# Group B of the trunk step: score tiles in the idle value ring, projection four slots sooner, second norm's statistics by column tile, new slot numbers

## The reference, cut to what matters

```python
sh1, sc1, gt1, sh2, sc2, gt2 = adaln(c, w_ada, b_ada)
h = rmsnorm(x, g_norm1) * (1.0 + sc1) + sh1
q, k, v, u, g = jnp.split(h @ w_in, IN_SPLITS, axis=-1)      # 2048 -> 5120 columns
u = gelu(u); vn = layernorm(gelu(g), ln_v_g, ln_v_b)
att, gate_v, states = mixer(q, k, v, vn)   # 8 heads of 128, dilated windows, ALiBi; samples read 2048 cached rows
x = x + gt1 * (concat([att, u * gate_v]) @ w_out)
h2 = rmsnorm(x, g_norm2) * (1.0 + sc2) + sh2
x = x + gt2 * peer_ffn(h2, w_query, sub_keys, expert_u, expert_v)
return rmsnorm(x, g_final), states
```

## Time and profile before

| | us |
| --- | --- |
| median of 3 runs | 3785.51 (3781.29 to 3787.98) |
| profiled execution, its own time | 3779.13 |
| its span, first to last instruction | 3777.4 |
| busy: PE / DVE / POOL / ACT | 3104.6 / 2353.0 / 980.1 / 572.1 |
| bytes moved by DMA | 1344.8 MB, mean 356 GB/s |
| mean granted TensorE clock | 0.903 |

### The profile page before, as it was taken

The page is one execution under the profiler, slowest core; times in us unless marked ns, Lnnn a source line. Parts: engine busy times, 40 slices in busy tenths (PEclk is TensorE's granted clock), DMA queues, the critical chain, the costliest instruction groups (busy, mean ns, idle before and its releaser), DMA issues.

```text
span 3777.4 us, 28728 instructions
## 1 busy us (share of the span) xinstructions
PE 3104.6 (82%) x9975; PEld 1850.8 (49%) x9975; DVE 2353.0 (62%) x3580; ACT 572.1 (15%) x1365; POOL 980.1 (26%) x779
## 2 busy tenths in 40 slices
PE   4899997979996668796885885359996589999996
PEld 1333443733343434333674553347773257777774
DVE  3110114889986854548777777877777838656653
ACT  0000111121111445402242000420000000000000
POOL 3000001234333421233313323333223314222220
PEclk8999998979998679897996997579998899999998
DMA  9999655889989799988989999889999989999993
GB/s 310 398 361 367 233 200 202 338 319 403 409 330 361 262 401 415 397 296 336 367 292 358 416 416 386 283 341 417 417 417 416 416 333 417 416 417 417 417 411 132
DMA packets 326129, 1344.80 MB, mean 356 GB/s; under 512 B 27625, under 2 KB 76777, under 8 KB 217593
## 3 DMA queue, kind: packets, MB, share of 16 engines
q0 software_dynamic: 106912, 749.72, 49.8%
q1 hardware_dynamic: 166090, 549.84, 37.9%
q10 hardware_dynamic: 52984, 43.42, 3.5%
HBM read 1303.07 MB, written 38.96 MB: 355 GB/s over the span
## 4 chain that ended last, share of the span: by engine, by line
PE 57%; DMA 20%; DVE 15%; issue 4%; ACT 3%; POOL 0%; SPq 0%; ACTq 0%; DVEq 0%; POOLq 0%
PE ps L1023 27%; PE ps L619 7%; DVE arena L2183 7%; DMA arena<-in_expert_u_dram,arena 6%; DMA arena<-in_expert_v_dram 5%; PE ps L778 4%; PE ps L828 4%; DMA arena<-in_cache_k_dram 3%; PE ps L710 3%; PE ps L577 2%; DMA arena<-in_w_ada_dram 2%; DMA arena<-in_w_in_dram 2%; PE ps L607 2%; PE ps L1015 2%; DMA arena<-in_w_out_dram 1%
## 5 line engine op out<-in xcount | busy, mean ns | idle before, releaser
L1023 PE MATMUL ps<-arena 128*128 128x512 f32 x3072 | 1384.4, 611 | 175.2 <-DMA arena<-in_expert_v_dram 116.1
L2183 DVE CUSTOM_DVE_ANT_0 arena<-arena 128x2048 f32<-128x2048 f32 x544 | 1241.7, 2290 | 315.3 <-DMA arena<-in_expert_u_dram,arena 309.5
L1023 PEld LDWEIGHTS ps<-arena 128*128 128x128 f32 x3072 | 943.6, 309 | 615.0 <-issue 270.9
L2448 POOL DMA_INDIRECT arena<-in_expert_u_dram,arena x544 | 760.6, 1398 | 1760.9 <-DVE arena L2183 1567.0
L2096 DVE SCALAR_TENSOR_TENSOR arena<-arena 128x2048 f32<-128x2048 f32 x158 | 371.6, 2352 | 205.3 <-issue 165.8
L828 PE MATMUL ps<-arena 128*128 128x512 f32 x896 | 409.4, 611 | 0.4 <-DVE arena L2027 0.2
L619 PE MATMUL ps<-arena 128*128 128x512 f32 x640 | 288.4, 604 | 9.5 <-DMA arena<-in_w_in_dram 9.5
L828 PEld LDWEIGHTS ps<-arena 128*128 128x128 f32 x896 | 169.7, 195 | 246.6 <-issue 240.1
L2448 POOL DMA_INDIRECT arena<-in_expert_v_dram,arena x160 | 176.7, 1105 | 410.5 <-DVE arena L2096 368.3
L577 PE MATMUL ps<-arena 128*128 128x128 f32 (+3 forms) x954 | 158.4, 319 | 151.7 <-DMA arena<-in_cache_k_dram 50.3
L577 PEld LDWEIGHTS ps<-arena 128*128 128x128 f32 (+3 forms) x954 | 128.0, 169 | 220.2 <-issue 67.7
(11 more groups left out here) (246 smaller groups left out, 1761.1 us busy)
## 6 DMA issues: line engine op xcount, KB each, us to landing
arena<-in_expert_v_dram SPq DMA_DIRECT2D x320, 512.0 KB
arena<-in_w_ada_dram SPq DMA_DIRECT2D x96, 1024.0 KB, 10.5
arena<-in_w_in_dram SPq DMA_DIRECT2D x80, 1024.0 KB, 8.2
arena<-in_w_query_dram SPq DMA_DIRECT2D x36, 1024.0 KB
arena<-dense_coefs SPq DMA_DIRECT2D x48, 768.0 KB
arena<-in_w_out_dram SPq DMA_DIRECT2D x32, 1024.0 KB, 5.1
dense_coefs<-arena ACTq DMA_DIRECT2D x12, 2048.0 KB, 20.4
arena<-in_cache_k_dram SPq DMA_DIRECT2D x24, 1024.0 KB
```

The lines of the kernel that those rows point to most:

```text
L1023: ins = MM(ps[:, BANK[half, b] + c, :], weights, dense_v[m % V_DENSE][:, c * NC:(c + 1) * NC], start=(m == FIRST_TILE[half, b]), stop=(m = ...
L2183: V.tensor_tensor_reduce(out=u_slot[s % RING], in0=u_slot[s % RING], in1=h2[b], scale=1.0, scalar=0.0, op0=ALU.mult, op1=ALU.add, accum_ou ...
L2448: nc.gpsimd.indirect_dma_start(out=slot, out_offset=None, in_=table, in_offset=bass.IndirectOffsetOnAxis(ap=idx, axis=0),).then_inc(loaded ...
```

## The change

- Block 0's scores of heads 2 to 7 go to R0 + 6 D and block 1's scores to R0 + 7 D, which are buffers of the `expert_v` ring that is idle until slot 408; heads 0 and 1 of block 0 go to `sc_first` at HB0. ACT's wait ahead of the "hb" turns drops from six heads' choices to two. Two other waits go (ACT in `mix_b`, SP ahead of a load of near values); one comes (ACT, before quad 8 of block 0 is copied into `stage`, for all choices of block 1, as the staging buffer lies over the scores).
- T_TURN1 and T_IN are 4 slots lower; all that hangs on T_IN moves with it.
- The choices of block 0 are due at 0, 4, 15, 21, 29, 37, 46, 55 in place of 0, 4, 17, 19.6, 23.2, 26, 36, 42; those of block 1 every 8 slots from 62 in place of every 7 from 52.
- A batch of `sample_keys` has 2.6 slots in place of 3.6, its key steps 0.3 apart in place of 0.4 (far ones from 1.4 in place of 2.0). The due times of `sample_values`, counted from the batch's end, stay as they were.
- `project_out` has 2.4 slots a quarter in place of 1.8; T_OUT goes from 202.75 to 191.75, T_NORM2 from 231.95 to 229.75, T_QB from 240.45 to 235.75.
- Second norm: `bn_stats` is taken of each column tile as it is added (into `delta`, which is free by then), and only the three `mean_square_end` stand at T_NORM2. The stores of x to `x_mid` are issued by ACT, three per column tile, in place of SP, three in all. The modulate calls are due 1, 2 and 3 slots after T_NORM2 in place of 4, 5 and 6.

```diff
-T_TURN1 = 30.0
-T_IN = 33.8
+T_TURN1 = 26.0
+T_IN = 29.8
 def t_key(n):
     h = n % H
-    return T_S + 2.0 + 3.6 * (n // H) + (0.4 * h if h < 4 else 2.0 + 0.4 * (h - 4))
+    return T_S + 2.0 + 2.6 * (n // H) + (0.3 * h if h < 4 else 1.4 + 0.3 * (h - 4))
-T_OUT = t_soft(DECB - 1) + 5.0
+T_OUT = t_soft(DECB - 1) + 6.0
 def t_out(n, q):
-    return T_OUT + 1.8 * (4 * n + q)
-T_NORM2 = t_out(OUT_T - 1, 3) + 2.2
-T_QB = T_NORM2 + 8.5
+    return T_OUT + 2.4 * (4 * n + q)
+T_NORM2 = t_out(OUT_T - 1, 3) + 2.0
+T_QB = T_NORM2 + 6.0
-TOP_0 = [0, 4.0, 17.0, 19.6, 23.2, 26.0, 36.0, 42.0]
+TOP_0 = [0, 4.0, 15.0, 21.0, 29.0, 37.0, 46.0, 55.0]
     if b == 1:
-        return 52 + 7.0 * h + piece
+        return 62 + 8.0 * h + piece
-        sc_sb = [at(off, PH, 2, NKEY) for off in (HB0, F0, MIX0, MIX0 + D, F0)]
-        sc_last = at(MIX0 + D + NC, 2, 2 * NKEY)
+        sc_sb = [at(off, PH, 2, NKEY) for off in (R0 + 6 * D, R0 + 7 * D, MIX0, MIX0 + D, F0)]
+        sc_first = at(HB0, 2, 2, NKEY)
@@ turns_b on ACT
-                        act.wait_ge(idx_ready, heads_of(0, PH - 2))
+                        act.wait_ge(idx_ready, heads_of(0, 2))
@@ mix_b on ACT
-                act.wait_ge(idx_ready, heads_of(0, PH))
@@ project_out on ACT
+                    yield t_out(n, 3) + 1.9
+                    act.wait_ge(outb_free, 2 * (n + 1))
+                    wait_turn_taken(act, ("of", n))
+                    cols = slice(n * NC, (n + 1) * NC)
+                    for i, b in enumerate((2, 3, SB)):
+                        act.dma_start(x1_of[b][:, cols], x_b[i][0:ROWS[b], cols]).then_inc(x1b_stored, 16)
@@ build_dense on ACT
+                        if n == 8:
+                            act.wait_ge(idx_ready, heads_of(1, PH))
@@ project_out on DVE
                         if b == SB:
                             turn_taken(ins, ("of", n))
+                            wait_turn_taken(dv, ("of", n))
                         else:
                             ins.then_inc(outb_free, 1)
+                            dv.wait_ge(outb_free, 2 * n + i + 1)
+                        link(V.bn_stats(out=st_b[i][0:r, 6 * n:6 * n + 6], in_=x_b[i][0:r, cols]))
+                yield T_NORM2
                 for i in range(3):
-                    yield T_NORM2 + i
-                    if i == 0:
...
-                    mean_square(7 + i, x_b[i])
+                    mean_square_end(7 + i, st_b[i])
                 for i in range(3):
-                    yield T_NORM2 + 4.0 + i
+                    yield T_NORM2 + 1.0 + i
                     if i == 0:
                         dv.wait_ge(mod2b_loaded, 64)
-                        dv.wait_ge(x1b_stored, 48)
+                        dv.wait_ge(x1b_stored, 48 * OUT_T)
@@ SP
                 else:
                     sp.wait_ge(u_done, SLOTS)
-                    sp.wait_ge(idx_ready, heads_of(1, PH))
...
-            sp.wait_ge(x1b_done, 1)
-            for i, b in enumerate((2, 3, SB)):
-                sp.dma_start(x1_of[b], x_b[i][0:ROWS[b], :]).then_inc(x1b_stored, 16)
```

More of the change, by code:

```diff
@@ L464, in trunk_step @@
         gate2_kept, gfin_kept, gate2_kept_s = at(MIX0, D), at(MIX0 + D, D), at(F0, D, rows=NS)
+        st_b = [delta[:, 24 * i:24 * i + 24] for i in range(3)]
         def heads_of(b, h):
@@ L1799, in _ @@
                 x1_tile(n, 0)
-            mean_square_end(2, 16)
+            mean_square_end(2)
             dv.sem_inc(x1a_done, 1)
```

34 lines of the change are left out of this document (15 added, 19 removed).

## The result

The changed kernel takes **3821.45 us** (median of 4 executions, 3814.17 to 3822.14) where the kernel before takes 3783.40 on the same chip (3776.54 to 3787.98): a ratio of 1.0098, 95% interval 1.0077 to 1.0118. It is 29 to 45 us slower. The profiled execution spans 3812.4 us, the one before 3777.4, both at a granted clock of 0.90.

A forecast was written before the change was run, and what follows sets the result against it. No engine was taken to bound the whole; what counts is when the stream reaches about slot 386. 23 - 11 - 4 + 12 - 14 + 8 = 14 us faster, 3771 us on the median's scale, range 3733 to 3797.

The forecast's parts named there:

- attention's first score product: Start to attention: PE reaches attention 23 us sooner (14 if nothing is gained, 32 if PE loses no weights wait).
- 14 of slots owed: After the first query, now at slot 235.75, not 240.45: 4.7 slots at about 3 us still to run, 14 us back.
- Projection 16 us sooner: Start of the projection on PE: at 788 to 789 us in place of 805.14, 16 us sooner.
- K and V are read back ... 13 us, as before: Between projection and attention: the read-back takes 13 us, as before, once PE is through.
- 29.3 us a batch: Sample batches: loop from `weigh` to `weigh`, 5.5 + 12.5 + 6 + 5.3; the output projection starts 11 us later against attention.
- all 2.6 gathers run beside them: Sample batches: if all 2.6 gathers run beside the far keys and values, the loop is 31.5 us.
- rival 1: Sample batches go by bytes at 24.2 us each: 23 instead of -11, so 48 us, 3737; chance 0.22.
- Seen by bytes: Sample batches: 10.1 MB in place of 11.1, 24.2 us in place of 27.2; 3 us less each, 23 in all.
- Output projection 4 us longer: Output projection: DMA now full too; 46 us for the first tile, 37 for each other, PE ends 4 us later.
- Second norm -12: Last output quarter to first query: first `modulate` at +13, not +25, 12 us saved (6 if stores land as slowly as before).
- Later -8: After the first query: block 2's first choice done sooner, 3 us; fewer query quarters between block 1's quads, 5 us.
- Rival 3: Sample batches: `weigh` behind the next batch's first key step makes a chain; loses above a 31.3 us loop; 3797; chance 0.18.

The follow-up runs named there:

- the hold: Changed kernel with POOL issuing slot 130's gather only after attention's two prompt blocks of keys and values are read back: 3818.14 us, ratio 1.0101.
- the projection's part: Kernel before with only the earlier turns and projection, scores in the value ring and choices spread out: 3784.76 us, ratio 1.0005.
- three pairs of runs: `weigh` late against first: changed kernel 3821.45 and 3789.07 us; new slot sharing only 3824.13 and 3791.15; kernel before 3808.74 (late) and 3779.73.
- With the order right: Kernel before with only the new sharing of slots, and `weigh` due between key steps 5 and 6: 3791.15 us, ratio 1.0019.
- with `weigh` first: Changed kernel with `weigh` and ACT's part of it due between the next batch's key steps 5 and 6: 3789.07 us, ratio 1.0020.
- the new sharing alone: Kernel before with only `t_key`, `T_OUT` and `t_out` as in the change, `weigh` staying late: 3824.13 us, ratio 1.0126.
- in the kernel before 1: Kernel before with only `weigh` and ACT's part of it due later, behind steps 6, 7 and the next 0: 3808.74 us, ratio 1.0088.
- the three-slot run: Kernel before with the second norm's part, and output projection quarters due every 2.0 slots, not 1.8: 3783.74 us, ratio 1.0015.
- Projection and norm together: Changed kernel with `t_key`, `T_OUT` and `t_out` as before, so without the new sharing of slots: 3800.63 us, ratio 1.0056.
- the norm's part alone: Kernel before with only `bn_stats` per tile, stores by ACT, and norm and query weights due earlier: 3773.26 us, ratio 0.9985.
- the one with the stores late: Kernel before with norm's part, new sharing, `weigh` between steps 5 and 6, and third tile's stores issued with the fourth's: 3781.19 us, ratio 0.9988.
- the kernel with norm and sharing: Kernel before with the norm's part, the new sharing and `weigh` between key steps 5 and 6: 3787.13 us, ratio 1.0019.
- the run with the output due sooner: Kernel before with norm's part, new sharing, `weigh` between steps 5 and 6, output projection due one slot sooner, 2.25 slots a quarter: 3785.31 us, ratio 1.0005.

## Where the prediction was right and where it failed

The forecast was 14 us faster, and it is 29 to 45 slower. Its sum, step by step, against the two traces:

| step of the sum | forecast, us | measured, us |
|---|---|---|
| attention's first score product | 23 sooner | 5.7 sooner |
| from there to the output projection | 11 longer | 17.1 longer |
| output projection, first to last quarter | 4 longer | 22.3 longer |
| last quarter to first query | 12 shorter | 6.1 shorter |
| first query to slot 288 (14 of slots owed, less 8) | 6 longer | 12.3 longer |
| slot 288 to slot 384 | nothing | 2.7 shorter |
| sum | 14 faster | 37.2 slower |

- **Projection 16 us sooner**: right, 788.23 for "788 to 789", last quarter 22.6 us sooner for 23. DVE's stalls at the gates of heads 2 and 3 too: 13.2 and 9.2 us for some 12 and 8.

```profile
740.51 0.16 DVE L1873 RECIPROCAL arena<-arena 128x1 f32<-128x1 f32 x1 [13.21 <-ACT arena L1216]
```

- **"K and V are read back ... 13 us, as before"**: failed on PE. It was 31.7 us from issue to turn, since the stream was no longer paused: 10 gathers issued beside the reads, 3 before. But the hold showed that this term is worth nothing to the end. The error beneath it is that the sum was kept on PE's clock. Taking 23 for the start and 12 of the 14 back for its four slots, the sum had the projection's part at -11; alone it measured +2 (-3 to +8). The price of 3 us a slot owed is fair but no law: first query's shift plus 3 us a slot owed gives slot 288 within 3 us in eight of the fifteen kernels (in the changed kernel 27.6 + 14 = 41.7, seen 39.9), and misses it by 5 to 11 us, in both directions, in the other seven.
- **The 8 batches, "29.3 us a batch"**: the chain was right, its size too small. Its legs were 5.5, 12.5 and 11.3 us; over six loops they measured 5.5, 14.8 and 11.1, so 31.4. The middle leg was counted with DMA full from 2 us behind `weigh`. It fills 2 us later:

```profile
1482.70:1484.70 2.00, 2.00 (x38) 1.04 (x40) 1.86 (x5) 0.00 (x0) 0.00 (x0) 1.00 0.33 61
1484.70:1500.60 15.90, 6.77 (x50) 3.27 (x42) 6.04 (x8) 4.99 (x11) 1.89 (x2) 0.87 1.00 414
```

  The one gather beside it (18.0% of the engines' time from 1486 to 1500 us) had been counted. That the loop came out at the 31.5 us of "all 2.6 gathers run beside them" is luck: one did.
- **The order's price** was right: between 29.3 us a batch and the 24.2 of rival 1 the forecast put 34 us in all (-11 against 23); three pairs of runs measure 32, 29 and 33 by medians. It is the main loss.
- **What failed is the gain that stood against the order.** "Seen by bytes" a gather less was to give 3 us a batch, 23 in all. The sum itself is off there: 27.2 us is taken at 408 GB/s and 24.2 at 417, and one gather of 1.05 MB is 2.5 us. With the order right seven loops gave 7 us in all (180 us for 187). I took a stage at 408 GB/s for one that only bytes bind; it sat where both bind, the bytes and the chain far keys, `weigh`, far keys. Removing bytes left the chain, and lengthening the chain left DMA idle.
- **Output projection 4 us longer**: failed, 22. Eleven of it comes with the order: with `weigh` first it is 156.8 us, not 167.6 (with the new sharing alone the order makes 6 us there, in the kernel before 1). In the late order the last two `weigh` are 11.5 us apart, not 17.5, and SP's issues in front of the first tile are held: the x tile's for 12.49 us (0.34 with `weigh` first), the sample rows' for 2.85 (0.43). That the 11 us come from these was not tested. The other 12 are the slots themselves, as the three-slot run shows. "So now it is full too" stood in the text, and its price was taken as 1.4 us a tile; it is 3 to 4.
- **Second norm -12**: in the changed kernel 6.1 (51.1 us for 57.1), alone 11.7 (45.4). The stores landed 8.4 to 9.0 us after a late issue. The section of the Trainium skill that the prediction draws on there (DMA: Bandwidth & Descriptors, "Anatomy of one DMA") tells of a DMA that GpSimd issues; these are ACT's, and no run here shows the fixed part alone. "On ACT the twelve issues ... some 2 us a tile, which nobody awaits" was wrong in both halves at the third tile: 5.72 us here, up to 29.61, with PE behind it.
- **Later -8**: not seen. Slot 288 is 39.9 late, as the first query and the slots alone say.

By parts, with their ratios on 3783 us: projection +2, norm -6, sharing +48, together +44, measured +37 (29 to 45). The forecast of the same parts: projection -11, norm -4, sharing +9, and -8 later. So the step that failed is the new sharing of slots: its batches and its output projection, forecast at 15 us on PE and measured at 39, where the cost of the order was seen and the gain set against it was not there. The projection's part comes second, 13 us short of its forecast. Rival 3 named the mechanism and set its turning point at a loop of 31.3; the loop was 31.4. But it priced the whole at 3797, as it left all other gains standing.

The parts do not simply add, though, and that the +44 lies so near the +37 is partly luck. Projection and norm together cost 21 us, not -4. Counted from there, the new sharing costs only 16 us by the ratios in the changed kernel (1.0098 against 1.0056), and with `weigh` first it even beats the old sharing (3789.07 against 3800.63), while alone with `weigh` first it loses 7. What holds in every setting tried is the order of `weigh`.

**Left open**: why the projection's and the norm's parts together cost 21 us (10 to 33) where each alone costs none. Its trace shows DMA idle 61 us between first query and slot 288, 47 in either part; the granted clock of that stretch is 0.82 there and 0.87 in either part, and DVE once waits 13.0 us for ACT ahead of a quad. Whether one of these is the cause was not tried. No version beats the kernel before beyond doubt; the norm's part alone (0.9985) and the one with the stores late (0.9988) come nearest.

## What to carry to other kernels

A stage that runs at full DMA may have a chain of issue, transfer and use that is just as long: before pricing bytes taken away, walk the loop once from the issue that repeats, and see what it costs with the bytes gone. When the slots of a stage are renumbered, look at every step whose place was given by an absolute offset: here 1.0 slot of spacing moved `weigh` behind two more far steps and the next batch's first, and that alone is 29 to 33 us by the medians. And sum on the resource that is owed at the end (DMA time not used), not on the engine whose steps moved: PE was through with the projection 22 us sooner with that part alone, and the whole gained nothing.

## What the runs showed of the hardware

Queues with work share the engines by packets, not by bytes. During the read-back in the changed kernel gathers had 1308 packets and the reads 1152, but 9.54 MB against 4.19, and 69.9% of the time against 31.5. Where both had work throughout, from 1172 to 1196 us, the counts are equal:

```profile
q0 software_dynamic: 912, 6.69, 67.1%
q1 hardware_dynamic: 911, 3.34, 34.5%
```

In the kernel with norm and sharing, from 1712 to 1718 us, three queues have work: the gathers (q0), SP's loads (q1) and ACT's stores (q10).

```profile
q0 software_dynamic: 259, 1.86, 73.4%
q1 hardware_dynamic: 258, 0.53, 22.5%
q10 hardware_dynamic: 260, 0.13, 7.3%
```

The Trainium skill (DMA: Bandwidth & Descriptors, "Queues, rings and completion order") says that a DMA engine takes a packet from each queue in turn; both traces agree. What that rule does to a kernel lies in the size of the packets: 7.3 KB each for gathers and 3.6 KB for the reads, so gathers got two thirds and the reads a third. The prediction's "up to half the engines" for gathers took the packets of both sides as equal.

An issue can hold its engine, and a full DMA alone does not do it. Three stores of a tile took ACT 5.7, 18.1 or 29.6 us at the third tile, but 1.29 at the fourth tile of the changed kernel, with DMA at 416 GB/s in the 10 us before:

```profile
1786.04 1.29 ACTq L1381 DMA_DIRECT2D x_mid<-arena  x3
```

What the held issues have in common is ACT's own queue. Eight quads' coefficients are stored by ACT too, 2 MB in packets of 512 bytes, some 4100 of them. In the kernel with norm and sharing that store was issued 22.7 us before the tile's and landed after 59.3 us:

```profile
1699.10 0.38 ACTq L1447 DMA_DIRECT2D dense_coefs<-arena  x1
```

When the third tile's stores came, 1791 of its packets were through (29.61 us held), 449 in the run with the output due sooner (18.10 us), 647 in the changed kernel (5.72 us). In the three-slot run all were through, and the issue took 1.32 us at 412 GB/s. In all eleven kernels whose stores ACT issues, three of them took 1.8 us or less unless such a store, or three stores just issued, stood in front. How long a hold lasts does not follow from the packets left, and no run moved the coefficients' store alone, so this cause is read from the rows and not shown by an experiment. SP's issue of one x tile took 12.49 us in the changed kernel and 0.34 before; what stood in its way was not looked into. The same page of the Trainium skill ("Rules for kernel authors") says that spreading DMAs over the issuing engines only saves issue time; here it moved a wait of up to 29.6 us onto an engine on which PE depends.
